# Weight casts later within a product, the next head's q scaled after the solve, and the mixer's last products begun with three of four heads

## The reference, cut to what matters

```python
def hybrid_mixer(h, w_in, ...):
    proj = h @ w_in
    u_f, u_sc, u_qkv, z, b_logit, a_logit, gate_logit = jnp.split(proj, idx, axis=-1)
    y_f = fourier_mix(u_f) @ w_fourier
    y_sc = short_conv_mix(u_sc, sconv_w) @ w_sconv_out
    y_dn = deltanet_branch(u_qkv, z, ...) @ w_dn_out
    gates = jax.nn.sigmoid(gate_logit).reshape(B, L, N_BRANCH, D)
    merged = gates[:, :, 0] * y_f + gates[:, :, 1] * y_sc + gates[:, :, 2] * y_dn
    return merged @ w_out
```

## Time and profile before

| | |
|---|---|
| median of 3 runs | 3009.8 us |
| profiled execution | 3016.0 us, its span 3014.7 us |
| TensorE busy | 2750.9 us (91%), 15982 instructions |
| TensorE weight loads | 2090.1 us (69%) |
| VectorE busy | 1224.6 us (41%) |
| ScalarE busy | 927.6 us (31%) |
| GpSimd busy | 161.5 us (5%) |
| mean granted clock of TensorE | 0.955 of full |
| the four heads of the delta rule | 1935 to 2498 us |
| mixer's end up to the first output tile | 2500 to 2547 us |

### The profile page before, as it was taken

How to read it: one execution, slowest core, us unless ns; L and a number is a source line. 1 busy time by engine, 2 the same in 40 slices (tenths; PEclk the granted TensorE clock), 3 DMA queues, 4 the chain that set the end, 5 groups by cost and what they waited for, 6 DMA issues and landing times. The chain is left out here.

```text
span 3014.7 us, 38051 instructions
## 1 busy us (share of the span) xinstructions
PE 2750.9 (91%) x15982; PEld 2090.1 (69%) x15982; DVE 1224.6 (41%) x2197; ACT 927.6 (31%) x1347; POOL 161.5 (5%) x219
## 2 busy tenths in 40 slices
PE   8999999997898889989999799798989898799997
PEld 6778888674433333379999787686868675578785
DVE  4456666444233333443333532343434334433334
ACT  4235554332111111142222431443434222431312
POOL 0000000000100000000000000303030300000000
PEclk9999999998899999999999899899999998899998
DMA  3022211225899999732222221211111112222221
GB/s 130 16 70 67 58 59 49 98 92 219 329 395 392 398 392 401 317 106 89 90 89 80 86 70 49 79 39 53 39 53 39 49 63 96 77 91 91 91 91 56
DMA packets 79082, 388.21 MB, mean 129 GB/s; under 512 B 9225, under 2 KB 9481, under 8 KB 53697
## 3 DMA queue, kind: packets, MB, share of 16 engines
q1 hardware_dynamic: 71856, 357.14, 33.2%
q0 software_dynamic: 6336, 26.73, 2.6%
q10 hardware_dynamic: 720, 1.90, 0.2%
HBM read 375.10 MB, written 10.62 MB: 128 GB/s over the span
## 5 line engine op out<-in xcount | busy, mean ns | idle before, releaser
L198 PE MATMUL ps<-uTr,ringr 128*128 128x512 f32 (+1 forms) x1408 | 415.8, 341 | 0.0
L198 PE MATMUL ps<-muh,ringr 128*128 128x264 f32 (+1 forms) x1504 | 384.1, 348 | 20.0 <-DVE uTr L478 11.9
L443 DVE TENSOR_TENSOR ringr<-ring,ringr 128x1024 fp32r<-128x1024 f32 (+1 forms) x215 | 258.5, 1211 | 252.7 <-ACT ringr L437 252.1
L198 PE MATMUL ps<-buh,ringr 128*128 128x512 f32 (+1 forms) x1312 | 350.3, 353 | 9.8 <-DVE oh L1235 4.3
L198 PE MATMUL ps<-fuh,ringr 128*128 128x264 f32 (+1 forms) x1296 | 283.3, 324 | 16.0 <-DVE ful L478 15.9
L198 PEld LDWEIGHTS ps<-muh,ringr 128*128 128x128 f32 x1504 | 253.1, 198 | 47.8 <-issue 17.5
L437 ACT CAST ringr<-ring 128x1024 fp32r<-128x1024 f32 (+1 forms) x215 | 219.9, 1037 | 160.2 <-DMA ring<-in_w_fi 37.2
L198 PEld LDWEIGHTS ps<-uTr,ringr 128*128 128x128 f32 x1408 | 247.5, 195 | 23.6 <-issue 3.1
L198 PEld LDWEIGHTS ps<-buh,ringr 128*128 128x128 f32 x1312 | 220.8, 190 | 42.8 <-issue 8.9
L198 PEld LDWEIGHTS ps<-fuh,ringr 128*128 128x128 f32 x1296 | 204.1, 191 | 39.6 <-issue 12.6
L198 PE MATMUL ps<-rmore,exT 128*64 128x512 f32 x736 | 181.5, 622 | 21.7 <-DMA rmore<-in_w_ein 20.2
(11 more groups left out here) (462 smaller groups left out, 4476.1 us busy)
## 6 DMA issues: line engine op xcount, KB each, us to landing
rmore<-in_w_ein SPq DMA_DIRECT2D x92, 1024.0 KB, 29.3
rmore<-in_w_eout SPq DMA_DIRECT2D x48, 1024.0 KB, 29.1
ring<-in_w_ein SPq DMA_DIRECT2D x36, 1024.0 KB, 29.3
ring<-in_w_fi SPq DMA_DIRECT2D x54, 512.0 KB, 3.7
fmore<-in_w_fi SPq DMA_DIRECT2D x34, 512.0 KB, 3.8
ring<-in_w_hg SPq DMA_DIRECT2D x32, 512.0 KB, 3.8
ring<-in_w_eout SPq DMA_DIRECT2D x16, 1024.0 KB, 29.6
ring<-in_w_out SPq DMA_DIRECT2D x32, 512.0 KB, 3.9
```

The lines of the kernel that those rows point to most:

```text
L198: return self.P.matmul(out, lhsT, rhs, start=start, stop=stop, skip_group_check=True)
L443: self.k.V.tensor_tensor(low, self.part(i), high.bitcast(F32), SUB).then_inc(self.rest.next(), 1)
```

## The change

Three things are moved; every engine issues the same instructions as before.

1. In the gates, z and the projections of heads 1 to 3, `ahead_act` stands four steps and `ahead_dve` five steps later in a product; for v behind q's silu and square on ScalarE, and behind k's scaling on VectorE.
2. `unit_dve("q", h, 1)`, the scaling of the next head's q to unit length, leaves the projection (except for head 0) and goes to the fourth step of the second gate tile (`gates_dve`).
3. In MixerEnd the fetch of the gates is issued when the last head no longer needs the memory under `mgb`; TensorE does not take part in the meeting of the engines any more; it multiplies the k-tiles of heads 0 to 2 for all eight output tiles into eight PSUM banks, then waits for head 3 and adds its k-tile to each; VectorE makes the two weights' low halves first, and a merged tile's low half two tiles behind its sum.

```diff
@@ Gates.act
         for j, what in enumerate("fs"):
+            for _ in range(4):
+                yield 1
             W.ahead_act(self.part[what, m])
-            for _ in range(7):
+            for _ in range(3):
                 yield 1
...
@@ project_act
         self.row_act("q", h, 1)
         yield 1
-        W.ahead_act(self.weights["v", h])
         yield 1
...
         self.silu_act("q", h, 1)
         self.square_act("q", h, 1)
+        W.ahead_act(self.weights["v", h])
@@ project_dve
         self.conv_dve("v", h, 2)
         yield 1
         yield 1
-        self.unit_dve("q", h, 1)
+        if h == 0:
+            self.unit_dve("q", h, 1)
         yield 1
+
+    def gates_dve(self, m):
+        h = m // 2 + 1
+        for s, step in enumerate(self.gates.dve(m)):
+            if m % 2 and h < 4 and s == 3:
+                self.unit_dve("q", h, 1)
+            yield step
@@ MixerEnd
+    def first_pool(self, net):
+        G = self.k.G
+        after(G, net.kk.at(8), net.qd_out.at(8), net.unit.at(8), self.gates.sent.last())
+        G.dma_start(self.gb[:, :, NM:L], self.gates.gd).then_inc(self.g_back.landing(), 16)
...
     def pe(self):
+        P.wait_ge(*heads.at(3))
         for m in range(8):
-            linear(k, b, tiles(kt(k.chunk(c)[:, o:o + 512], 4), 4), self.dn, 0, S).then_inc(self.prod.next(), 1)
+            for t in range(3):
+                k.mm(k.ps[:, b, :], w[m][t], self.dn[:, t, :], t == 0, False)
+        P.wait_ge(*heads.at(4))
+        for m in range(8):
+            k.mm(k.ps[:, b, :], w[m][3], self.dn[:, 3, :], False, True).then_inc(self.prod.next(), 1)
...
     def dve(self):
-        for m in range(8):
-            V.wait_ge(*self.prod.at(m + 1))
...
         W.rest_dve(0)
         W.rest_dve(1)
-        for m in range(8):
-            self.pm.low_dve(k.hT[:, m, NM:L], k.uh[:, m, NM:L], k.ul[:, m, NM:L], m, scale=0.5)
+        for m in range(10):
+            if m < 8:
+                V.wait_ge(*self.prod.at(m + 1))
...
+            if m >= 2:
+                n = m - 2
+                self.pm.low_dve(k.hT[:, n, NM:L], k.uh[:, n, NM:L], k.ul[:, n, NM:L], n, scale=0.5)
@@ mixer
-            k.join(*net.sigs, gates.sent, k.spilled)
+        end.first_pool(net)
+        for eng in (k.V, k.A, k.G):
+            after(eng, *(s.last() for s in net.sigs + [gates.sent, k.spilled]))
```

More of the change, by code:

```diff
@@ L2630, in act @@
             yield 1
-        for _ in range(8):
+        for _ in range(8 + 4):
             yield 1
         W.ahead_act(self.part["d", m])
-        for _ in range(7):
+        for _ in range(3):
             yield 1
@@ L2643, in dve @@
         for what in "fs":
+            for _ in range(5):
+                yield 1
             W.ahead_dve(self.part[what, m])
-            for _ in range(8):
+            for _ in range(3):
                 yield 1
@@ L3058, in project_act @@
         k, A, W = self.k, self.k.A, self.W
+        late = 4 if h else 0
+        for _ in range(late):
+            yield 1
         W.ahead_act(self.weights["k", h])
-        for _ in range(7):
+        for _ in range(7 - late):
             yield 1
@@ L3065, in project_act @@
         yield 1
+        for _ in range(4):
+            yield 1
         W.ahead_act(self.weights["q", h])
-        for _ in range(5):
-            yield 1
+        yield 1
         self.silu_act("k", h, 0)
@@ L3175, in dve @@
         for h in range(4):
-            fill.rest += self.stream(h, self.z_dve, self.gates.dve, self.project_dve)
+            fill.rest += self.stream(h, self.z_dve, self.gates_dve, self.project_dve)
             self.prepare_dve(h, fill)
@@ L3210, in project_dve @@
         W = self.W
+        late = 5 if h else 0
+        for _ in range(late):
+            yield 1
         W.ahead_dve(self.weights["k", h])
-        for _ in range(8):
+        for _ in range(8 - late):
+            yield 1
+        self.conv_dve("k", h, 0, *([self.kk.at(2 * h)] if h else []))
+        for _ in range(5):
             yield 1
         W.ahead_dve(self.weights["q", h])
-        self.conv_dve("k", h, 0, *([self.kk.at(2 * h)] if h else []))
-        for _ in range(8):
+        for _ in range(3):
             yield 1
-        W.ahead_dve(self.weights["v", h])
         self.conv_dve("q", h, 1)
@@ L3223, in project_dve @@
         self.unit_dve("k", h, 0)
-        for _ in range(4):
+        yield 1
+        W.ahead_dve(self.weights["v", h])
+        for _ in range(3):
             yield 1
@@ L3382, in pe @@
     def pe(self):
-        k, P = self.k, self.k.P
+        k, P, heads = self.k, self.k.P, self.net.dn_out
+        last = self.net.bank["osum", 3]
+        banks = [b for b in (4, 5, 6, 7, 0, 1, 2, 3) if b != last] + [last]
+        w = [tiles(kt(k.chunk(self.chunk0 + m // 4)[:, 512 * (m % 4):512 * (m % 4) + 512], 4), 4) for m in range(8)]
+        P.wait_ge(*heads.at(3))
         for m in range(8):
-            c = self.chunk0 + m // 4
             if m % 4 == 0:
-                P.wait_ge(*k.there(c))
-            self.bank["d", m] = b = k.pair()
-            o = 512 * (m % 4)
-            linear(k, b, tiles(kt(k.chunk(c)[:, o:o + 512], 4), 4), self.dn, 0, S).then_inc(self.prod.next(), 1)
-            k.give((b, b + 1), self.gated.at(m + 1))
+                P.wait_ge(*k.there(self.chunk0 + m // 4))
+            self.bank["d", m] = b = banks[m]
+            k.take(b)
+            for t in range(3):
+                k.mm(k.ps[:, b, :], w[m][t], self.dn[:, t, :], t == 0, False)
+        P.wait_ge(*heads.at(4))
+        for m in range(8):
+            b = banks[m]
+            k.mm(k.ps[:, b, :], w[m][3], self.dn[:, 3, :], False, True).then_inc(self.prod.next(), 1)
+            k.give((b,), self.gated.at(m + 1))
         for m in range(8):
@@ L3484, in mixer @@
             net.pool()
[L3485 to L3487 removed]
+        k.sig.close(kept + nxt.sigs + net.sigs + [net.kk, net.qd_out, net.unit, gates.sent, k.spilled])
+        end = MixerEnd(k, st, dn, gates, net, gain(k, 3), nxt)
+        end.first_pool(net)
+        for eng in (k.V, k.A, k.G):
+            after(eng, *(s.last() for s in net.sigs + [gates.sent, k.spilled]))
         end.sp()
```

21 lines of the change are left out of this document (9 added, 12 removed).

## The result

The changed kernel takes **2928.8 us** (median of 4 runs, 2927.1 to 2930.6) against 3010.2 of the kernel before beside it: ratio 0.9727, 95% interval 0.971 to 0.9744, 81 us less. The forecast was 2931, range 2920 to 2957. The profiled execution took 2927.7, its span is 2926.4: 88.3 less than the span before. Of the 27 runs of the kernel before that were taken beside the experiments one took 3171.2 us, at a mean clock of 0.82, and is left out of what follows.

What follows compares the result with a forecast made beforehand. TensorE bounds the kernel (91% busy), losing time to waits and half clock. 19.2 + 12.6 + 9.2 + 33 + 4.9 = 78.9 us off the profiled 3016.0 gives 2937.1, less 6.2 to the median: 2931 us, range 2920 to 2957.

Steps and rivals of the forecast that it cites:

- Decays, 19.2 us: Decay stages of four heads: later casts remove TensorE's waits on nDT and nTT, 7.7 + 13.4 less 1.9 us.
- casts in the recurrence, 12.6: Recurrence: of 17.3 us waits on nKK the three long ones go, 12.6 us; thirteen of about 0.35 us stay.
- the length of four steps: Four k-tile steps last 2.8 us back to back, 4.6 us in the recurrence, behind the load's 4.0 us.
- Solve, 9.2: Solve, three heads: q's scaling moved away, 12.5 us of nTT waits less 3.3 (about 1.1 us stay each).
- Elsewhere a cast of 1.05 us only changes its place in ScalarE's queue: Casts outside decay and recurrence: moving them costs nothing, as their products are wanted more than 5.6 us later.
- Clock, 33: Four heads: low clock follows the waits, so 33 us of work at half clock is saved; the largest term.
- the 4 us that were taken off: Clock term: 37 us cut to 33 for new low stretches behind 1.1 us waits and 75 rather than 79 found.
- the first rival's condition: Clock stays up behind the remaining waits and under VectorE's pace: 2924 us, chance 0.12.
- Mixer's end, 4.9: Mixer's end: first output product done 4.9 us sooner; 7.6 without the low clock, 2 if it lasts twice as long.
- 2.7 us more: Mixer's end: low clock expected while VectorE sets the pace, costing 2.7 us, moving 2539.1 to 2541.9.
- Signs named beforehand: Four heads: nTT and nDT waits under 3 us together, nKK under 6, clock 0.98 or more; end: no mdn wait.
- Short waits on uTr of L478 adding to 5 to 7 us: Mixer's end: sign of a right forecast, TensorE's short waits on uTr of L478 adding up to 5 to 7 us.

Runs made afterwards that it cites:

- u2: Changed kernel with all casts of gates, z, q, k and v back at the first step of each product: 2974.8 us.
- v4: Changed kernel with casts of gates, z, k and q two steps late on ScalarE, three on VectorE, instead of four and five: 2929.8 us.
- v7: Changed kernel with casts of gates, z, k and q one step late on ScalarE, two on VectorE, instead of four and five: 2953.6 us.
- v8: Changed kernel with the gates' casts alone back at their early places; z, q, k and v as changed: 2983.1 us.
- u1: Changed kernel with q's scaling put back at the end of the projection; casts and mixer's end as changed: 2948.2 us.
- v1: Changed kernel with ScalarE's cast of v's weights ahead of q's silu and square instead of behind them: 2924.7 us.
- v2: Changed kernel with the gates' products at the mixer's end taking PSUM banks in the order 0, 1, 4, 5, 6, 7, 2, 3: 2927.6 us.
- v3: Changed kernel with v's cast ahead of q's silu, v2's bank order, and v's silu moved from the solve into the next gates' steps: 2927.4 us.
- a0: The changed kernel run once more, unaltered: 2928.7 us.

## Why the prediction was right, point by point

- **Decays, 19.2 us, and casts in the recurrence, 12.6.** The waits went, and more fully than foreseen: no 0.35 us stays on nTT, and ten waits of 0.19 us on nKK stay instead of thirteen of 0.35. From before to after 7.7 + 13.4 + 15.4 = 36.5 us went where the sum had 31.8. The working had misread the nKK line: of its 16 waits ten are the short ones of head 3 (0.18 to 0.19 each), and three more stand near the end of the other heads' recurrences, behind an early low half on VectorE:

```profile
2072.29 0.46 PE L198 MATMUL ps<-nDT,nKK 88*128 88x88 f32 x2 [0.93 <-DVE nKK L3294]
```

These three (0.93, 0.92, 0.92) went too. u2 brings back 34.8 us of the waits on these three results; its 31.3 is what is left when the 3.6 on nCP go. What the working had wrong is the reason for the length of four steps: it counted 4.6 us in the recurrence against 4.0 us of landing, where two steps do as well (v4), and in the decays it is the order on VectorE, not the time, that frees nTT (v7). And it held every cast to be at fault, where the gates' alone are enough for the long waits (v8).
- **Solve, 9.2.** u1 prices it at 9.6; the rest on ScalarE's copy behind v's silu is 0.95 us, foreseen as 1.1.
- **Not in the sum:** the 3 x 1.2 us on nCP. The sentence "Elsewhere a cast of 1.05 us only changes its place in ScalarE's queue" is a step that failed: v's cast went behind q's silu and square, and its half on VectorE, which stands ahead of nCP, went with it. The term should have been -3.6 (v1).
- **Idle time in sum:** 52.3 - 10.0 = 42.3 beside 41.0. That is luck: 4.7 us too little for the casts and 3.6 too much for the wait that v's cast made nearly cancel.
- **Clock, 33.** Measured 510.7 - 475.0 = 35.7. The condition, that the low clock follows the waits, is shown by u1 and u2. Of the 4 us that were taken off, the half for 75 us at the low clock in place of 79 was right. The other half, for new low stretches behind waits of 1.1 us, was not needed: in the heads there were none behind 1.20 and 0.95, in either trace of the changed kernel. There the first rival's condition held, and with it the page of the Trainium skill that it named ("TensorE: Matmul & The Clock Gate", section "What's actually happening"), by which idleness is the state of the low clock. It did not hold everywhere: behind the last head's square TensorE waits 1.00 us in all 14 traces, and in 13 of them the clock was low there. A length that decides can't be read from these traces: every wait of 3.04 us or more in the heads of u1, u2, v7 and v8 had half clock behind it, and among the shorter ones u2's 1.61, v7's 1.89 and two of v7's three of 2.99 had, v8's 2.25 and 2.73, v7's 1.98 and 2.02 and the last of 2.99 had not.
- **Mixer's end, 4.9.** Measured 7.1 to 7.4. First tile 23.0 us after the sum (22.7 forecast), 16.8 from there to the copy: 39.7. The forecast had 15.6 + 0.8 for TensorE's last k-tile there; on VectorE it is 15.5 and then the 1.2 of L443 ahead of the copy, which the forecast didn't list. The forecast's 41.9 has 2.7 us more, and that term is the one that failed: the low stretch came (2454.9 to 2458.3), but it lay beside VectorE's chain, for which TensorE had to wait anyway. u1 and v7 show it, with the same banks and a clock of 1.00 there. This is u1's stretch from 9 to 17 us behind the first gate, and then the changed kernel's:

```profile
2474.00:2482.00 8.00, 6.50 (x26) 4.73 (x27) 7.78 (x13) 3.79 (x5) 0.55 (x1) 1.00 0.02 7
```
```profile
2453.40:2461.40 8.00, 7.55 (x26) 6.02 (x27) 7.76 (x13) 3.78 (x5) 0.55 (x1) 0.79 0.01 5
```

In u1 and v7 TensorE then waits 1.0 us for VectorE's low halves, and from the first gate to ScalarE's last copy it is 55.8 and 55.7 us, as in the changed kernel (55.8). So this low stretch cost nothing. A longer one does: v2's, of some 7 us, cost 1.3. The bank pair was not foreseen and cost nothing either. So the gain went past the prediction's "4.9 or less", although the clock fell as expected.
- **Signs named beforehand:** nTT and nDT under 3 us, nKK under 6, clock 1.00, VectorE's waits on casts 33.9 us in 14 against 105.1 in 27, no wait for mdn: all as said. Short waits on uTr of L478 adding to 5 to 7 us: not seen; one of 3.40 on the gate stood there, and with the banks of v2 and v3 they appear, at 2.5 and 3.8.
- **From the profiled execution to the median:** between the two profiled spans the kernel gained 88.3 us where the sum said 78.9: 1.3 more in idle time, 2.7 in the clock, 2.4 at the end, 2.8 by chance after the mixer. Between the medians it gained 81.4, because the kernel before had been profiled 6 us above its median. The forecast, set down from that median by the sum, came out 2 us off because what it missed and what the profiled execution had too much of nearly cancel. That it is so close is luck: single terms were off by up to 4.7 us.

## What to carry to other kernels

A wait shows under the name of the result that is late, and the instruction to move is the one that stands ahead of it in its engine's program order; look up in the code which call issues it, since a helper that works ahead issues it under another product's step. Move no more than that: each instruction moved lands ahead of something else, as v's low half did. And price a wait at its length plus the clock behind it when it is long: here 4.18 us in place of 0.95 cost 7.3 (u1), while the waits of 1.2 us in the heads cost only themselves. That holds for their place, not for their length: the wait of 1.00 us at the last head's end did have a low clock behind it.

## What the runs showed of the hardware that I had not expected

- Waits at the same place and of the same length are not followed by the same clock. v2 and v3 have the same order of products at the mixer's end and short waits on the same results; TensorE's clock was 0.51 in one and 1.00 in the other. Behind a wait of 4.2 us in the recurrence it was low for some 3.5 us in u2's head 0, and behind one of 4.1 for some 7 us in v8's.
- Two traces of one kernel differ by 1.7 us in 80 at the mixer's end (80.8 and 79.1), where only the granted clock differs: half clock for 3.4 us behind the last head's square (a wait of 1.00 us) in one, not in the other. Here are the two stretches, the changed kernel's and a0's:

```profile
2420.00:2424.00 4.00, 3.83 (x6) 1.61 (x7) 0.00 (x0) 3.81 (x5) 0.00 (x0) 0.62 0.21 78
```
```profile
2421.00:2425.00 4.00, 3.65 (x9) 1.73 (x10) 0.00 (x0) 3.94 (x5) 0.00 (x0) 1.00 0.00 1
```

a0 is the exception. In u1 and v7 the clock was low for some 7 us there, and their ends are 1.3 us longer than the changed kernel's.
- A GpSimd addition of 128x512 floats took 1.26 us on its first and 1.68 and 1.67 on its next two uses, and VectorE's addition beside it 1.06 to 1.36 us in place of 0.69, where GpSimd's had begun first. The three that were slower each ended 0.5 to 0.6 us behind GpSimd's. VectorE's gates, which read one operand from PSUM, kept their 0.68 beside it. Its low halves kept 0.68 too, but they had begun before GpSimd's addition (2449.24 against 2449.39, 2452.74 against 2452.90), and there it was GpSimd's that took 1.68 and 1.67 in place of 1.26. So with these instructions the one that began second was slower. Whether the gates were spared for their PSUM operand, no run here tests.
